# Expert 0's rows gathered before the last token tile is routed, completed by selection products

## What is computed

```
t = rmsnorm(x2)                               # 520 x 1024
group  = argmax(t @ w_router_group)           # 1 of 4 groups
two    = top_k(softmax(expert logits of that group), 2)
for e in range(32):
    out += combine[:, e] * ((silu(t @ w_gate[e]) * (t @ w_up[e])) @ w_down[e])
y = rmsnorm(x2 + out)
```

## Time and profile before

| | us |
|---|---|
| median of 3 runs (721.83 to 722.79) | 722.72 |
| the profiled execution's own time | 723.84 |
| its span in the trace | 722.1 |

### The profile page before, as it was taken

How to read it: one execution, slowest core, us unless ns; L and a number is a source line. 1 busy time by engine, 2 the same in 40 slices (tenths; PEclk the granted TensorE clock), 3 DMA queues, 4 the chain that set the end, 5 groups by cost and what they waited for, 6 DMA issues and landing times.

```text
span 722.1 us, 9235 instructions
## 1 busy us (share of the span) xinstructions
PE 648.2 (90%) x3176; PEld 312.2 (43%) x3176; DVE 255.8 (35%) x554; ACT 158.6 (22%) x312; POOL 98.0 (14%) x165
## 2 busy tenths in 40 slices
PE   8999999999999899996899999997787777878895
PEld 4478878874456433332233333332222222223331
DVE  7798998188265612111010101010001100001047
ACT  3677611142322111110011111110001010001033
POOL 4100001000000311212012121212211112112000
PEclk9999999999999999998999999999999999999998
DMA  9532004869858699999999999999999999999993
GB/s 323 229 117 99 19 1 171 309 225 430 319 148 308 216 424 423 425 425 421 429 424 424 426 421 423 423 425 425 422 427 427 423 424 428 426 421 427 396 345 124
DMA packets 32692, 244.48 MB, mean 339 GB/s; under 512 B 7344, under 2 KB 8016, under 8 KB 19584
## 3 DMA queue, kind: packets, MB, share of 16 engines
q1 hardware_dynamic: 25592, 233.95, 79.0%
q0 software_dynamic: 5280, 8.24, 3.1%
q10 hardware_dynamic: 1768, 1.53, 0.7%
HBM read 235.76 MB, written 17.09 MB: 350 GB/s over the span
## 4 chain that ended last, share of the span: by engine, by line
PE 64%; DMA 12%; DVE 11%; another core or an unknown queue 5%; ACT 3%; issue 2%; SPq 1%; POOLq 0%; POOL 0%; DVEq 0%
PE psA L1495 33%; PE psB L1495 29%; DMA mem<-in_w_gu 7%; DVE mem L790 5%; DMA mem<-y_d 2%; DMA mem<-x_d,mem 1%; DVE mem L1014 1%; PE psB L1500 1%; DMA mem<-in_w_vb 1%; PE psA L1500 1%; ACT front_c L713 1%; DMA y_d<-mem 1%; ACT mem L721 1%; DVE mem L929 1%
## 5 line engine op out<-in xcount | busy, mean ns | idle before, releaser
L1495 PE MATMUL psA<-mem 128*128 128x260 f32 (+9 forms) x863 | 201.6, 471 | 9.0 <-DMA mem<-in_w_down 6.3
L1495 PE MATMUL psB<-mem 128*64 128x512 f32 (+8 forms) x715 | 153.4, 486 | 14.3 <-DMA mem<-in_w_down 4.9
L1495 PEld LDWEIGHTS psA<-mem 128*128 128x128 f32 (+5 forms) x863 | 109.0, 159 | 84.1 <-issue 61.4
L1495 PE MATMUL psB<-mem,front_c 128*64 128x512 f32 (+3 forms) x554 | 121.2, 577 | 15.6 <-DMA mem<-in_w_gu 15.6
L1495 PE MATMUL psA<-mem,front_c 128*64 128x512 f32 (+2 forms) x548 | 119.2, 575 | 13.6 <-DMA mem<-in_w_gu 12.1
L1495 PEld LDWEIGHTS psB<-mem 128*64 128x64 f32 (+5 forms) x715 | 73.8, 160 | 78.5 <-issue 57.1
L1495 PEld LDWEIGHTS psB<-mem,front_c 128*64 128x64 f32 (+2 forms) x554 | 41.2, 142 | 93.9 <-issue 67.8
L1495 PEld LDWEIGHTS psA<-mem,front_c 128*64 128x64 f32 (+1 forms) x548 | 40.3, 140 | 89.7 <-issue 68.8
L790 DVE TENSOR_TENSOR mem<-mem 128x512 f32<-128x512 f32 (+17 forms) x114 | 66.4, 600 | 23.7 <-ACT mem L620 19.6
L1189 DVE SCALAR_TENSOR_TENSOR front_c<-psB,tiny,front_c 64x512 f32<-64x512 f32 x16 | 12.1, 755 | 176.8 <-ACT front_c L713 170.2
L1189 DVE SCALAR_TENSOR_TENSOR front_c<-psA,tiny,front_c 64x512 f32<-64x512 f32 x16 | 12.1, 756 | 176.2 <-ACT front_c L713 163.6
(11 more groups left out here) (252 smaller groups left out, 375.8 us busy)
## 6 DMA issues: line engine op xcount, KB each, us to landing
mem<-in_w_gu SPq DMA_DIRECT2D x62, 2048.0 KB, 35.3
mem<-in_w_down SPq DMA_DIRECT2D x29, 2048.0 KB, 42.8
mem<-in_w_down SPq DMA_DIRECT2D x5, 1024.0 KB, 8.7
mem<-in_w_out SPq DMA_DIRECT2D x2, 2048.0 KB, 8.3
y_d<-mem SPq DMA_DIRECT2D x1, 4096.0 KB, 12.6
mem<-y_d SPq DMA_DIRECT2D x8, 512.0 KB, 8.2
mem<-in_w_gu SPq DMA_DIRECT2D x6, 512.0 KB, 3.8
mem<-in_x_T SPq DMA_DIRECT2D x8, 260.0 KB, 8.9
```

The costliest lines, as they stand in the source:

```text
L1495: return nc.tensor.matmul(out, lhsT, rhs, start=start, stop=stop, skip_group_check=True)
```

## The change

Expert 0's rows are found in two parts. As soon as the first four tiles (0, 4, 1, 2: 392 rows) are placed, 16 small products sum expert 0's column of the table for them, VectorE makes the row numbers (first_row), and POOL gathers these rows into xg[:, 0], which it has set to zero before. Once tile 3 is routed, VectorE makes a selection matrix first_rows (128 rows of tile 3 x 64 slots, one where the row sits in that slot of expert 0). TensorE multiplies the gathered rows by the identity, which transposes them into PSUM, and adds on top the rows of tile 3 in SBUF times first_rows. The rows' roots are completed in the same way.

Around this:
- SP waits for the early gather before it issues the last two issues of blocks (7, 2 to 4 and 10, 3: 1.5 MB), and for xgT_ps, the end of the selection products, before block (9, 3).
- The 8 sample rows stand in x2_d, y2_d and picks at rows 384 to 391 and tile 3 behind them (BASE), so that the early gather reads one range.
- POOL gathers expert 1's rows behind tbl_rdy and tile 3's stores (last_out), then already expert 2's.
- VectorE computes the bounds xb before the table, and the chain of the further tiles' table and expert 1's copy move behind expert 0's two copies.
- TensorE runs further_table after six of expert 0's eight steps (before them only if expert 0 has more than 64 rows), turns expert 1's rows at the end of expert 0's products rather than halfway, and runs last_weights after six steps of expert 1; 15 of the keep_busy products go.
- ScalarE waits for xslot_rdy 1 instead of xtbl_rdy before its loop; two pairs of semaphores are merged.

The core of the diff:

```diff
@@ SP
+            sp.wait_ge(xg_in[0], 16)
             load_blocks(7, 2, 4)
             load_blocks(10, 3, 4)
-            sp.wait_ge(x2_out, 16 * (NT + 1))
-            sp.wait_ge(xg_in[0], 16)
+            sp.wait_ge(last_out, 16 * 3)
+            sp.wait_ge(xgT_ps, 1)
             load_blocks(9, 3, 4)
@@ VectorE
             add_half(1)
+            dve.wait_ge(first_ps, 1)
+            high, row, less = (first_ids[:, k:k + 1] for k in range(3))
+            link(V.tensor_scalar(high, psA[:, 0, 0:1], 16.0, row_base, ALU.mult, ALU.add))
+            link(V.scalar_tensor_tensor(row, psA[:, 0, 1:2], 2.0, high, ALU.mult, ALU.add))
+            link(V.tensor_scalar(less, row, float(2 * NTOK), float(-2 * NTOK), ALU.is_ge, ALU.mult))
+            tt(first_row, less, row, ALU.add).then_inc(first_rdy, 1)
             root(4, 3)
             top_two(4, 3)
+            dve.wait_ge(oh_rdy, NT)
+            link(V.tensor_scalar(not_first, ohb[:, 3, 0:1], -4096.0, 4096.0, ALU.mult, ALU.add))
+            dve.wait_ge(pre_ps, 5)
+            V.scalar_tensor_tensor(first_rows, rank_at, not_first, psA[:, 1, 32 * 4:32 * 4 + 1].to_broadcast([128, C]),
+                                   ALU.add, ALU.is_equal).then_inc(first_rdy, 1)
             place(4, 3)
...
             V.tensor_copy(xb[0:1, 1:NE + 1], xs[0:1]).then_inc(xslot_rdy, 1)
+            dve.wait_ge(first_ps, 2)
+            first_xT_copy(0, first_rdy)
+            dve.wait_ge(tbl_ps, 1)
+            rows_of(tbl, psA[:, 3, :], NE)
+            dve.wait_ge(xgT_ps, 1)
+            tt(root_of[:, 0:1], xg[:, 0, DE:DE + 1], psB[:, 0, 0:1], ALU.add)
+            first_xT_copy(1, xgT_ev)
...
             rows_of(tblx, psA[:, 3, 128:512], NX + 1).then_inc(xtbl_rdy, 1)
             dve.wait_ge(xtbl_rdy, 1)
+            tile_step(0, 0, early=True)
             dve.wait_ge(ex_out, 1)
...
-            tile_step(0, 0, early=True)
             tile_step(1, 1)
@@ POOL
-            pool.wait_ge(x2_out, 16 * (NT + 1))
-            pool.wait_ge(root_out, 16 * NT)
-            pool.wait_ge(tbl_rdy, 1)
+            pool.wait_ge(o_ps, NT + 1)
+            link(G.memset(xg[:, 0, :], 0.0))
+            pool.wait_ge(x2_out, 16 * (NT - 1))
+            pool.wait_ge(root_out, 16 * (NT - 1))
+            pool.wait_ge(first_rdy, 1)
...
-            fetch_first(0)
-            fetch_first(1)
+            fetch_first(0, first_row, 2 * BASE[3])
+            pool.wait_ge(tbl_rdy, 1)
+            pool.wait_ge(last_out, 16 * 3)
+            fetch_first(1, tbl[:, 1, 0:1])
+            pool.wait_ge(xgT_ev, 1)
+            fetch(2, 0)
@@ TensorE
             turn_half(0)
+            pe.wait_ge(slot_rdy, 4)
+            for n, t in enumerate(ORDER[0:4]):
+                r = ROWS[t]
+                for j in range(2):
+                    for g in range(2):
+                        ins = mm(psA[C * g:C * g + C, 0, 0:2], row_oh[0:r, t, j, :], entry[0:r, t, j, 0, :],
+                                 n == 0 and j == 0, n == NT - 2 and j == 1)
+            ins.then_inc(first_ps, 1)
             turn_half(1)
             logits_half(0)
             logits_half(1)
-            pe.wait_ge(slot_rdy, 4)
...
-            keep_busy(2)
+            def first_rows_of(h):
+                for j in range(4):
+                    ins = mm(psA[:, 2 * h, C * j:C * j + C], x2[:, 3, DE * h + 128 * j:DE * h + 128 * j + 128], first_rows, False, True)
+                return ins
+            pe.wait_ge(xg_in[0], 16)
+            for j in range(4):
+                for h in range(2):
+                    mm(psA[:, 2 * h, C * j:C * j + C], xg[:, 0, 128 * j:128 * j + 128], ident[:, C * h:C * h + C], j == 0, False)
+            pe.wait_ge(first_rdy, 2)
+            first_rows_of(0).then_inc(first_ps, 1)
             pe.wait_ge(slot_rdy, NT)
             table_rows(3, False, True)
-            pe.wait_ge(tbl_rdy, 1)
+            for g in range(2):
+                mm(psB[C * g:C * g + C, 0, 0:4], first_rows, x2_root[:, 3, :], True, True)
+            first_rows_of(1).then_inc(xgT_ps, 1)
...
-            keep_busy(8)
             pe.wait_ge(xslot_rdy, 1)
-            x0, x1 = bound(0), bound(1)
-            keep_busy(5)
-            pe.wait_ge(xg_in[0], 16)
-            x_T(psA[:, 0, :], xg[:, 0, :]).then_inc(xgT_ps, 1)
-            further_table()
...
-            x0, x1 = tile_step(0, x0, x1, before=False, halfway=other_half)
+            x0, x1 = tile_step(0, 0, bound(1), before=False, ahead=further_table,
+                               between={4: lambda: pe.wait_ge(xgT_ev, 1), 6: further_table})
...
-            x0, x1 = tile_step(1, x0, x1, halfway=last_weights)
+            x0, x1 = tile_step(1, x0, x1, between={6: last_weights})
```

More of the change, by code:

```diff
@@ L1229, in tile_step @@
                     xT_copy(s + 1, 1 - u)
[L1231 to L1240, removed]
             dve.wait_ge(xtbl_ps, 1)
@@ L1415, in wait_before, with fetch_first @@
                 pool.wait_ge(signal, count)
-            def fetch_first(s):
-                gather(xg[:, s, :], tbl[:, s, 0:1]).then_inc(xg_in[s], 16)
+            def fetch_first(s, rows, *count):
+                gather(xg[:, s, :], rows, *count).then_inc(xg_in[s], 16)
             def fetch(s, u):
@@ L1618, in y_wave, with sums @@
                 ins.then_inc(y_ps, 1)
-            def sums(sq, ready, done):
+            def sums(sq, ready):
                 pe.wait_ge(ready, 5)
@@ L1762, in x_T, with gate_up @@
                 return ins
-            def gate_up(out, xT, e, half=None, halfway=None):
+            def gate_up(out, xT, e, half=None, between={}):
                 for k in range(KD):
-                    if k == 4 and halfway:
-                        halfway()
+                    if k in between:
+                        between[k]()
                     unit, count = place_of(e, k // 4)
@@ L1806, in used_further, with further @@
                 wait_before(xx_y, n)
-            def further(x0, x1, ps, other, e, n_xT=0, n_h=0, turned=False):
-                with pe.If(x0 < x1), pe.Fori(x0, x1) as x:
+            def further(x0, x1, ps, other, e, n_xT=0, n_h=0, turned=False, ahead=None):
+                with ExitStack() as inside:
+                    inside.enter_context(pe.If(x0 < x1))
+                    if ahead:
+                        ahead()
+                    x = inside.enter_context(pe.Fori(x0, x1))
                     if not turned:
@@ L1840, in bound, with tile_step @@
                 return pe.value_load(xb[0:1, k:k + 1], min_val=0, max_val=NX)
-            def tile_step(s, x0, x1, before=True, halfway=None):
+            def tile_step(s, x0, x1, before=True, between={}, ahead=None):
                 u = s % 2
@@ L1848, in tile_step @@
                 else:
-                    pe.wait_ge(xgT_half, 1)
-                further(x0, x1, ps, other, s, n_h=s)
-                gate_up(ps[:, 1, :], xgT[:, u], s, half=gu_half, halfway=halfway).then_inc(gu_ps, 1)
+                    pe.wait_ge(first_rdy, 3)
+                further(x0, x1, ps, other, s, n_h=s, ahead=ahead)
+                gate_up(ps[:, 1, :], xgT[:, u], s, half=gu_half, between=between).then_inc(gu_ps, 1)
+                if not before:
+                    turn_rows(s + 1)
                 if before:
@@ L1907, in turn_h @@
                 h_T(psA[:, 2, :], hh[0:64, 0, :]).then_inc(hT_ps, 1)
[L1909 removed]
+            gate_up(psB[:, 1, :], xgT[:, 1], NE - 1, between={4: turn_h}).then_inc(gu_ps, 1)
             pe.wait_ge(hT_ev, NE - 1)
```

91 lines of the change are left out of this document (48 added, 43 removed).

## The result

The changed kernel takes 725.77 us (median of 5 runs, 723.76 to 726.73) against 722.72 (5 runs beside them): ratio **1.0036 [1.0024, 1.0049]**. Forecast was a gain of 4.0 us; it is a loss of 3. The profiled execution took 725.85 (span 724.1) against 723.84.

What follows compares the result with a forecast made beforehand. The 32 experts' weight DMA at 425 GB/s was taken as the bound. Unused DMA time from 228 to 253 would fall from 11.1 to 7.1 us, gaining 4.0: 718.7 against 722.72, range 716.8 to 721.9.

Steps and rivals of the forecast that it cites:

- its currency: Before the expert loop: what happens before 260 us counts only by the DMA time it leaves unused, 11.1 us from 228 to 253.
- The early ids: TensorE and VectorE after tile 3's half sum: sixteen two-column products take 0.5 us, four operations end at 229.8, 0.15 delay.
- POOL's issue: POOL issues expert 0's early gather at 230.8 instead of 238.31.
- What stands in line behind expert 0: Table just in time at 245.0, VectorE's reads 1.65 us, second gather adds nothing; expert 1 at 249.8, 1.5 us earlier.
- the selection products: TensorE before expert 0: sixteen identity entries from 235.4 take 1.9 us, halves end at 238.2 and 239.5; expert 0 at 240.0.
- rival A: Expert 1 starts late or the clock falls, stretching expert 0's products by 1.7 us: gain only 1 to 3; chance 0.27.
- the row nearest is the empty queue: landing at 234.0: Expert 0's early gather lands 3.2 us after issue, as with an empty queue; ends 233.7 and 241.2.
- rival B: At SP's new wait: a gather landing after 235.4 costs one us per us, break-even 239.4, slowest 724.5; chance 0.08.
- list of signs of being wrong: Landing after 235.4, clock 0.50 after 240, expert 1 set by its gather, or last weights landing no earlier.
- 425 GB/s after that: DMA behind the first whole refill unit, issued near 253.4, runs at 425 GB/s.
- the forecast's 7.1: DMA time lost from 228 to 253 with the change: 7.1 us against 11.1 before.
- the full 4.0: Whole kernel: a gain of 4.0 us, to 718.7 against the median of 722.72.

Runs made afterwards that it cites:

- experiment 9: experiment 6 with the first 0.5 MB of unit 7 issued ahead of the early gather and 2 MB behind it: 719.90 us, ratio 0.9963 to the kernel before.
- experiment 2: The changed kernel with the held 1.5 MB of blocks issued ahead of SP's wait for the early gather again: 724.54 us, ratio 1.0016 to the kernel before.
- experiment 5: The changed kernel with all 2.5 MB held behind the early gather and keep_busy(10) for keep_busy(6) before the last count: 720.58 us, ratio 0.9965 to the kernel before.
- experiment 7: The kernel before with only its 15 keep-busy products around expert 0 (2, 8 and 5) left out: 724.25 us, ratio 1.0017.
- experiment 1: The changed kernel with keep_busy(9) for keep_busy(6) before the last count and keep_busy(4) behind the total count: 722.20 us, ratio 0.9989 to the kernel before.
- experiment 4: experiment 1 with expert 1's rows turned after six of expert 0's eight steps instead of behind them: 722.58 us, ratio 0.9998 to the kernel before.
- experiment 6: experiment 5 with expert 1's rows turned early and VectorE's two reads moved ahead of its wait for the table: 720.69 us, ratio 0.9971 to the kernel before.
- experiment 8: experiment 4 with VectorE's two register reads moved ahead of its wait for the further tiles' table: 721.35 us, ratio 0.9983 to the kernel before.
- experiment 10: experiment 6 with SP released when POOL has sent the early gather, not when it has landed: 719.75 us, ratio 0.9965 to the kernel before.
- 11: experiment 6 with both 0.5 MB ahead of the gather and 2 MB released once the gather is sent: 720.43 us, ratio 0.9965 to the kernel before.
- 3: The changed kernel with block (7, 0 to 2) also held, so all 2.5 MB go behind the early gather: 723.18 us, ratio 0.9993 to the kernel before.

## Why the prediction was wrong

**Right.** What bounds the kernel, and its currency: unused DMA time and run time moved together. In the thirteen profiled executions unused ranges from 7.7 (experiment 9) to 15.1 us (experiment 2), and the time less unused lies between 711.6 and 712.8 in all of them. The early ids: the sixteen two-column products took 0.59 us (said 0.5), the last of the four operations ended at 229.76 (said 229.8), and VectorE still waited 1.35 us behind them. POOL's issue: 230.75 (said 230.8). What stands in line behind expert 0: the table just in time, VectorE's reads 1.80 us (said 1.65), and, in experiment 5, the second gather adding nothing to expert 1.

**Wrong 1, the selection products: "16 f32 entries, at the 0.12 us of the router products 1.9 us" and eight each for the halves.** The price came from a row at full clock; at full clock it was right to 0.15 us (2.00, 1.06, 1.10). The step that failed is the one that weighed rival A: "Against it: the selection products fill TensorE nearly without a gap". They do, and the clock was low all the same, because it had fallen ahead of them; the sum put the clock at nothing. The fillers in the wait before, and what follows them, from TensorE's timeline of the kernel before and of experiment 7, whose code is the same up to here:

```profile
231.83 2.93 PE L1495 MATMUL psB<-ident 128*128 128x128 f32 x12
...
231.79 1.60 PE L1495 MATMUL psB<-ident 128*128 128x128 f32 x12
234.74 0.48 PE L1495 MATMUL psA<-mem 128*128 128x32 bf16 x5 [1.35 <-DVE mem L790]
```

The first row is of before, the other two of experiment 7. In the profile of before, at low clock, the twelve entries lasted 2.93 us and covered the wait up to 234.70; at full clock the same twelve took 1.60 and left 1.35 idle, in experiment 7 as in the changed kernel. So it was not the change that made them fast: their number had covered the wait only in an execution that was at low clock there. New with the change are the missing fillers behind them and the landing, which left another hole behind 235.46. The clock then stayed low through the 64-column products, with TensorE busy 6.00 of 6.00 us from 240 to 246. Rival A had the mechanism. The Trainium skill's "TensorE: Matmul & The Clock Gate" (HAM oscillation), named there, speaks for it, and the trace now agrees: 10.3 us at 0.50, from within the second wait on. But A's price was one stretch, 1.7 us, upon expert 0's products alone. Measured between the changed kernel and experiment 1 it is 3.5 us ahead of expert 0 and 1.0 in its products (6.38 against 5.37). Shown by experiments 1 and 7; and in the profiles of all eight versions with the further fillers (1, 4, 5, 6, 8 to 11) the clock is 1.00 in every window from 228 to 260, in the four without them (the changed kernel, 2, 3, 7) it falls to 0.50 between 236.0 and 238.2.

**Wrong 2, "the row nearest is the empty queue: landing at 234.0".** The queue was not empty: 1 MB stood ahead, and none of the earlier trace rows shows that case. The sum over all DMA engines was nearly right (drained by 234), but the wait is for the last engine, and that one had half of its part of the block and its part of tile 3's store to move ahead of the gather's last rows. The landing was 5.8 us; with 1 MB in flight 3.7 (experiment 4) to 6.4 (1), with none or 0.5 MB 2.9 to 3.4 (3, 5, 6, 9 to 11), with 2.5 MB 6.9 (2). The packet records of the other profiles with 1 MB fit: one such engine in experiment 8 (up to 235.60), two in 1 (up to 235.45 and 236.49), none past 234.5 in 4. The landing moved the first identity product from 235.4 to 236.58, 1.2 us. By rival B's own price that takes 1.2 us off the gain and makes no loss; the forecast weighed late landing and low clock one at a time, and both came. Its list of signs of being wrong names both: a landing after 235.4 and a clock of 0.50 after 240. Shown by experiments 2, 3 and 5.

The two account for expert 0: 240.0 + 1.2 + 3.5 = 244.7; the products' true length of 4.1 us at full clock, where the working left 4.6, takes 0.5 off, and the trace has 244.21.

**Wrong 3, smaller: "425 GB/s after that".** With both mended (experiment 5, which holds 1 MB more) the windows from 228 to 253 leave 7.3 us unused, the forecast's 7.1; but those from 253 to 400 leave another 1.1 (401 and 423 GB/s). No version gained the full 4.0; the best median is 3.4 us below its before (experiment 10), by the ratio 2.5.

**Still open.** Which DMA engine is the last, and why one or two of them fall 1 to 2 us behind the others, or none, with the same 1 MB ahead. What in a stream of products lifts the clock: experiments 1 and 5 show that fillers ahead keep it, not which property of them does. And whether every execution of the changed kernel has the dip: one profile shows it, and the five runs' mean clocks (0.982 to 0.987, against 0.985 to 0.993 in experiment 1) fit.

## What to carry to other kernels

When a change fills or shortens a wait, look at what TensorE does in that wait: filler products are part of the timing of what comes behind them, and removing or speeding them up can cost more than the wait was worth. Price a new small DMA by what the last engine still has to move ahead of it, not by the mean bandwidth; bulk transfers issued right behind it did it little harm here (experiment 10). And before moving work off a chain, see what its next wait is: where the DMA is already nearly full (experiment 6), an earlier start bought nothing.

## What was not expected of the hardware

TensorE was busy without a pause for nearly ten us and stayed at 1.2 GHz: 0.50 from 236.0 to 246.3, through 3.67, 1.91 and 1.97 us of 64-column products and the first two us of 512-column ones. A gather of 32 packets with rows landed some 2.5 us after the mean DMA share had fallen to 0.08, because one engine of 16 still had 12 other packets to move ahead of the gather's last two. And two register reads with a branch held VectorE for 1.80 us, more than any of its operations in this stretch (at most 0.83 in the changed kernel).
